# A transformer layer with mixture of experts: the first ada columns on TensorE, x turned and projected in two halves

## The reference

```
c_act = silu(c)                                   # 1024 values
mod   = c_act @ ada_w + ada_b                     # 1024 x 6144: sh1, sc1, g1, sh2, sc2, g2
z     = rmsnorm(x, norm1_g) * (1 + sc1) + sh1
xa, ya, u, v = split(z @ w_in, 4)                 # w_in 1024 x 2048, 512 columns each
o_lru = rg_lru(xa, gelu(ya)) ; o_sgu = sgu(gelu(u), gelu(v))
h     = x + g1 * (concat(rmsnorm(o_lru), rmsnorm(o_sgu)) @ w_out)
z2    = rmsnorm(h, norm2_g) * (1 + sc2) + sh2
h     = h + g2 * moe(z2)                          # 32 experts, top 4, 1024 -> 2048 -> 1024
out   = rmsnorm(h, final_g)
```

## Time and profile before

| | us |
|---|---|
| median of 3 runs | 2230.58 |
| lowest and highest | 2229.54, 2233.26 |
| the profiled execution, its own time | 2232.91 |
| its span in the profile | 2231.2 |
| TensorE busy | 2001.2 |
| VectorE, GpSimd, ScalarE busy | 992.8, 538.4, 356.3 |
| mean granted clock of TensorE | 0.955 of full speed |

### The profile page before, as it was taken

How to read it: one execution, slowest core, us unless ns; L and a number is a source line. 1 busy time by engine, 2 the same in 40 slices (tenths; PEclk the granted TensorE clock), 3 DMA queues, 4 the chain that set the end, 5 groups by cost and what they waited for, 6 DMA issues and landing times.

```text
span 2231.2 us, 51505 instructions
## 1 busy us (share of the span) xinstructions
PE 2001.2 (90%) x20191; PEld 827.5 (37%) x20192; DVE 992.8 (44%) x2237; ACT 356.3 (16%) x723; POOL 538.4 (24%) x530
## 2 busy tenths in 40 slices
PE   3988989976999999999998689969999998999994
PEld 3443444432433343433433123413334332434341
DVE  6436645334444444444444233434444443444444
ACT  3025311221101111101011111111010111110112
POOL 2000022032232323232232222232223232232222
PEclk9998999987999999999999889979999999999997
DMA  9222216250536718673599999799999569955355
GB/s 333 97 110 86 85 55 189 113 195 29 182 106 254 255 28 294 227 247 117 180 391 400 399 402 400 253 379 399 391 401 382 197 226 405 387 191 191 96 183 181
DMA packets 128670, 526.37 MB, mean 236 GB/s; under 512 B 17120, under 2 KB 47840, under 8 KB 79488
## 3 DMA queue, kind: packets, MB, share of 16 engines
q1 hardware_dynamic: 95344, 470.39, 53.9%
q0 software_dynamic: 33296, 55.61, 10.8%
HBM read 493.55 MB, written 32.38 MB: 236 GB/s over the span
## 4 chain that ended last, share of the span: by engine, by line
PE 60%; DMA 11%; SPq 2%; issue 1%; DVE 1%; DVEq 1%; ACT 0%; POOLq 0%
PE psum L1106 39%; PE psum L1124 21%; DMA big<-in_exp_w_gu_dram 9%; SPq L426 1%; DMA big<-in_exp_w_down_dram 1%; DVEq L348 1%; DVE r L1655 0%; PE psum L1058 0%; SPq L436 0%; SPq L433 0%; PE psum L1070 0%; DMA acc_rows<-r,scatter_idx 0%; DMA r<-acc_rows 0%; DVE r L1522 0%; DMA r<-hs_rows,gather_idx 0%
## 5 line engine op out<-in xcount | busy, mean ns | idle before, releaser
L1106 PE MATMUL psum<-big,r 128*32 128x512 f32 x9152 | 1023.0, 604 | 53.2 <-DMA big<-in_exp_w_gu_dram 48.3
L1106 PEld LDWEIGHTS psum<-big,r 128*32 128x32 f32 x9152 | 298.1, 111 | 736.3 <-issue 649.8
L1124 PE MATMUL psum<-big,r 128*32 128x256 f32 x9152 | 529.7, 388 | 44.4 <-DVE r L1605 21.6
L611 POOL DMA_INDIRECT acc_rows<-r,scatter_idx x143 | 226.5, 1584 | 945.9 <-DVE r L1613 928.1
L1124 PEld LDWEIGHTS psum<-big,r 128*32 128x32 f32 x9152 | 301.5, 112 | 251.2 <-issue 47.4
L796 ACT ACTIVATE r<-r,shift 128x128 f32<-128x128 f32 x384 | 157.4, 480 | 1074.5 <-PE psum L1106 891.9
L1590 DVE TENSOR_TENSOR r<-psum,r 128x256 f32<-128x256 f32 x143 | 60.4, 423 | 412.9 <-PE psum L1106 412.7
L603 POOL DMA_INDIRECT r<-hs_rows,gather_idx x196 | 193.8, 989 | 87.0 <-issue 44.7
L1610 DVE TENSOR_TENSOR r<-psum,r 128x256 f32<-128x256 f32 x143 | 60.8, 425 | 339.8 <-PE psum L1124 339.5
L874 PE MATMUL psum<-r,big 128*128 128x512 f32 x384 | 167.9, 598 | 1.3 <-DMA big<-in_w_in_dram 1.3
L803 ACT ACTIVATE r<-r 128x256 f32<-128x256 f32 x143 | 59.6, 417 | 418.3 <-DVE r L1596 416.2
(11 more groups left out here) (233 smaller groups left out, 983.7 us busy)
## 6 DMA issues: line engine op xcount, KB each, us to landing
big<-in_exp_w_gu_dram SPq DMA_DIRECT2D x256, 1024.0 KB
big<-in_exp_w_down_dram SPq DMA_DIRECT2D x128, 1024.0 KB
big<-in_ada_w_dram SPq DMA_DIRECT2D x12, 2048.0 KB, 12.8
r<-in_x_dram SPq DMA_DIRECT2D x16, 512.0 KB, 12.5
big<-in_w_in_dram SPq DMA_DIRECT2D x4, 2048.0 KB, 19.0
r<-in_exp_b_gu_dram SPq DMA_DIRECT2D x128, 64.0 KB
big<-in_w_out_dram SPq DMA_DIRECT2D x2, 2048.0 KB, 13.3
hs_rows<-r POOLq DMA_DIRECT2D x8, 512.0 KB, 3.0
```

Of the source, the lines that this page charges most:

```text
L611: pool.indirect_dma_start(acc_quarters, bass.IndirectOffsetOnAxis(ap=scatter_idx[:, u:u + 1], axis=0), y_sb[:, u, :], None, bounds_check=4 ...
L1106: last = pe.matmul(psum[32 * j:32 * j + 32, u, :].rearrange("p (a n) -> p a n", a=2), izT[:, k, u * UNIT:(u + 1) * UNIT], rhs[:, :, 256 * ...
L1124: ins_ = pe.matmul(psum[32 * i:32 * i + 32, 4 + u % 2, 0:256], actT[:, u, f, :], down_slab(f)[:, 256 * i:256 * i + 256], start=(f == 0), s ...
```

## The change

- The ada tiles 0 to 3 are replaced by four pairs: pair j holds rows 256 j to 256 j + 255 of the first 2048 columns, in rows of 8 KB, in the same slot of the ring. TensorE multiplies them: the stationary operand is `cact_cols`, 32 columns of which the first is silu(c) and the rest zero (GpSimd's memset), and the four groups of 512 columns go into the four 32-partition parts of one bank. `gemv_made` is counted by TensorE after each of the pairs 0 to 2, and once more at the next job. VectorE copies the bank; four small matmuls (`mods`) turn its four rows into 16 columns, and VectorE adds ada_b.
- SyncE issues x 0 to 3, then w_in 0, then x 4 to 7, then ada 4.
- ScalarE squares four tiles of x (into `x_sq`, in `r2`), evicts its half of zT of the first half of tokens, and then does the same for the second half.
- TensorE turns the first half of x, projects xa of the first half, turns the second half and projects it.
- VectorE scales x 0 between its two steps on mod, x 1 to 3 after `scale1`, evicts, scales x 4 to 7, copies the four xa banks of the first half and evicts the second half. The copies of the second half stay where the copies were, with the convolution and the products of ada 4 and 5 between them.

```diff
--- before.py
+++ after.py
@@ -69,10 +69,10 @@
 
 def bank_jobs():
 
-    jobs = [("cols", 0, "dve")]
-    jobs += [("mod", j, "dve") for j in range(4)]
-    jobs += [("zT", (k, th), "dve" if k % 2 else "act") for th in range(2) for k in range(KT)]
-    jobs += [("xa", (m, th), "dve") for m in range(CT) for th in range(2)]
+    jobs = [("cols", 0, "dve"), ("ada", 0, "dve"), ("mods", 0, "dve")]
+    for th in range(2):
+        jobs += [("zT", (k, th), "dve" if k % 2 else "act") for k in range(KT)]
+        jobs += [("xa", (m, th), "dve") for m in range(CT)]
     jobs += [("mod", j, "dve") for j in (4, 5)]
     jobs += [("g1row", q, "dve") for q in range(2)]
     jobs += [("wm", q, "dve") for q in range(2)]
@@ -157,6 +157,9 @@
         def ring(key):
             return big[:, DENSE_AT[key] % DENSE_SLOTS, :].rearrange("p (k n) -> p k n", k=8)
 
+        def ada_pair(j):
+            return big[:, j, :].rearrange("p (k n) -> p k n", k=2)
+
         lru_t = big[:, 4, :].rearrange("p (i n) -> p i n", i=4)
         s5 = big[:, 5, :]
         ln_g = s5[:, 0:512]
@@ -167,6 +170,7 @@
         wi_bd = s5[:, 3072:3584].rearrange("p (c n) -> p c n", c=CT)
         router_w = s5[:, 3584:3840].rearrange("p (k e) -> p k e", k=KT)
 
+        x_sq = r2[:, 5120:6144]
         zT = r1[:, :].rearrange("p (k n) -> p k n", k=KT)
         h_rows = r1[:, :].rearrange("p (t n) -> p t n", t=TT)
 
@@ -219,7 +223,8 @@
         before = lru_t[:, 0, 0:P]
         prow = r2[:, 0:P]
         cols = sb("cols", [P, NROWS])
-        cact = sb("cact", [P, KT])
+        cact_cols = sb("cact_cols", [P, KT, UNIT])
+        cact = cact_cols[:, :, 0]
         mod = sb("mod", [P, 48])
         scale1 = sb("scale1", [P, KT])
         affine2 = sb("affine2", [P, 2, KT])
@@ -402,8 +407,8 @@
                 sp_.dma_start(prow[ROW[name]:ROW[name] + rows, :], src.rearrange(pat, p=P)).then_inc(param_in, SEMW)
 
             for n, (kind, j) in enumerate(DENSE):
-                if n == DENSE_SLOTS:
-                    for t in range(TT):
+                if n in (DENSE_SLOTS, DENSE_SLOTS + 1):
+                    for t in range(4 * (n - DENSE_SLOTS), 4 * (n - DENSE_SLOTS) + 4):
                         sp_.dma_start(x_rows[:, t, :], x[t * P:(t + 1) * P, :]).then_inc(x_in[t], SEMW)
                 if n >= DENSE_SLOTS:
                     old, i = DENSE[n - DENSE_SLOTS]
@@ -412,6 +417,11 @@
                     else:
                         last = ("v", TT - 1) if i == 3 else (("xa", "ya", "u")[i], (CT - 1, 1))
                         sp_.wait_ge(filled, JOB[last] + 1)
+                if n < DENSE_SLOTS:
+
+                    sp_.dma_start(ada_pair(j), ada_w[2 * P * j:2 * P * (j + 1), 0:2048].rearrange("(k p) n -> p k n", p=P)
+                                  ).then_inc(dense_in[n], SEMW)
+                    continue
                 w = {"ada": ada_w, "win": w_in, "wout": w_out}[kind]
                 sp_.dma_start(ring((kind, j)), w[:, j * 512:(j + 1) * 512].rearrange("(k p) n -> p k n", p=P)
                               ).then_inc(dense_in[n % DENSE_SLOTS], SEMW)
@@ -491,6 +501,7 @@
                 ins_.then_inc(pool_chain, 1)
                 pool.wait_ge(pool_chain, chain[0])
 
+            link(pool.memset(cact_cols[:, :, :], 0.0))
             link(pool.memset(ident[:, :], 0.0))
             link(pool.affine_select(out=ident[:, :], in_=ident[:, :], compare_op=ALU.not_equal, fill=1.0, base=0,
                                     pattern=[[-1, P]], channel_multiplier=1))
@@ -667,16 +678,17 @@
 
             act.wait_ge(const_made, 1)
             act.wait_ge(dve_drained, 1)
-            act.activation(cact[:, :], cols[:, ROW["c"]:ROW["c"] + 8], ACT.Silu).then_inc(cact_made, 1)
-
-            for t in range(TT):
-                act.wait_ge(x_in[t], SEMW)
-                link(act.activation(r1[:, 0:D], x_rows[:, t, :], ACT.Square, accum_out=ssum[:, t:t + 1]))
-                act.activation(srt[:, t:t + 1], ssum[:, t:t + 1], ACT.Sqrt, bias=eps[:, 0:1], scale=1.0 / D
-                               ).then_inc(sqrt_made, 1)
-
-            act.wait_ge(affine_made, 1)
+            act.activation(cact, cols[:, ROW["c"]:ROW["c"] + 8], ACT.Silu).then_inc(cact_made, 1)
+
             for th in range(2):
+                for t in range(4 * th, 4 * th + 4):
+                    act.wait_ge(x_in[t], SEMW)
+                    link(act.activation(x_sq, x_rows[:, t, :],
+                                        ACT.Square, accum_out=ssum[:, t:t + 1]))
+                    act.activation(srt[:, t:t + 1], ssum[:, t:t + 1], ACT.Sqrt, bias=eps[:, 0:1], scale=1.0 / D
+                                   ).then_inc(sqrt_made, 1)
+                if th == 0:
+                    act.wait_ge(affine_made, 1)
                 for k in range(0, KT, 2):
                     b = take("zT", (k, th))
                     act.activation(zT[:, k, th * 512:(th + 1) * 512], b, ACT.Identity, bias=mod[:, SH1 + k:SH1 + k + 1],
@@ -880,8 +892,24 @@
             pe.wait_ge(const_made, 1)
             b = open_bank("cols", 0)
             pe.transpose(b[:, 0:NROWS], prow[0:NROWS, :], ident[0:NROWS, 0:NROWS]).then_inc(filled, 1)
-            for j in range(4):
-                mod_cols(j)
+            b = open_bank("ada", 0)
+            pe.wait_ge(cact_made, 1)
+            for n in range(4):
+                dense_ready(("ada", n))
+                for kk in range(2):
+                    k = 2 * n + kk
+                    for i in range(4):
+                        last = pe.matmul(b[32 * i:32 * i + 32, :], cact_cols[:, k, :], ada_pair(n)[:, kk, 512 * i:512 * i + 512],
+                                         start=(k == 0), stop=(k == KT - 1), skip_group_check=True)
+                last.then_inc(gemv_made if n < 3 else filled, 1)
+            b = open_bank("mods", 0)
+            wait_drained(pe, JOB[("ada", 0)])
+            for i in range(4):
+                last = pe.matmul(b[:, 4 * i:4 * i + 4], gacc[:, 0, i * P:(i + 1) * P], ident[:, 0:P:UNIT],
+                                 start=(i == 0), stop=True, skip_group_check=True)
+                if i == 0:
+                    last.then_inc(gemv_made, 1)
+            last.then_inc(filled, 1)
 
             for th in range(2):
                 pe.wait_ge(x_scaled, 4 * th + 4)
@@ -890,11 +918,10 @@
                     for i in range(4):
                         last = pe.transpose(b[:, i * P:(i + 1) * P], x_rows[:, 4 * th + i, k * P:(k + 1) * P], ident[:, :])
                     last.then_inc(filled, 1)
-            dense_ready(("win", 0))
-            for who, drained in (("act", act_drained), ("dve", dve_drained)):
-                pe.wait_ge(drained, drained_before(JOB[("zT", (KT - 1, 1))], who))
-            for m in range(CT):
-                for th in range(2):
+                dense_ready(("win", 0))
+                for who, drained in (("act", act_drained), ("dve", dve_drained)):
+                    pe.wait_ge(drained, drained_before(JOB[("zT", (KT - 1, th))], who))
+                for m in range(CT):
                     project("xa", ("win", 0), m, th)
             for j in (4, 5):
                 mod_cols(j)
@@ -1213,7 +1240,7 @@
 
                 n = DENSE_AT[("ada", j)]
                 dve.wait_ge(dense_in[n % DENSE_SLOTS], SEMW * (n // DENSE_SLOTS + 1))
-                if j >= 2:
+                if j >= 6:
 
                     dve.wait_ge(filled, JOB[("mod", j - 2)] + 1)
                 w, a = ring(("ada", j)), gacc[:, j % 2, :]
@@ -1230,16 +1257,20 @@
                 dve.tensor_tensor(mod[:, 4 * j:4 * j + 4], b[:, 0:4], col("ada_b", 4 * j, 4), ALU.add
                                   ).then_inc(dve_drained, 1)
 
+            def scale_x(t):
+
+                dve.wait_ge(sqrt_made, t + 1)
+                link(dve.reciprocal(rstd[:, t:t + 1], srt[:, t:t + 1]))
+                dve.tensor_scalar(x_rows[:, t, :], x_rows[:, t, :], rstd[:, t:t + 1], None, ALU.mult).then_inc(x_scaled, 1)
+
             dve.wait_ge(cact_made, 1)
-            mod_products(0)
-            mod_products(1)
-            mod_add(0)
-            mod_products(2)
-            mod_add(1)
-            mod_products(3)
-            mod_add(2)
-            mod_add(3)
-            dve.wait_ge(dve_drained, drained_by(JOB[("mod", 3)])[1])
+            b = take("ada", 0)
+            dve.tensor_copy(gacc[:, 0, :], b).then_inc(dve_drained, 1)
+            scale_x(0)
+            b = take("mods", 0)
+            dve.tensor_tensor(mod[:, 0:16].rearrange("p (i b) -> p b i", b=4), b[:, 0:16].rearrange("p (b i) -> p b i", b=4),
+                              col("ada_b", 0, 16).rearrange("p (i b) -> p b i", b=4), ALU.add).then_inc(dve_drained, 1)
+            dve.wait_ge(dve_drained, drained_by(JOB[("mods", 0)])[1])
             link(dve.tensor_scalar(scale1[:, :], mod[:, SC1:SC1 + 8], 1.0, None, ALU.add))
             dve.tensor_tensor(scale1[:, :], scale1[:, :], col("norm1_g", 0, 8), ALU.mult).then_inc(affine_made, 1)
```

(20 more changed lines are left out.)

## The result

| | before | after |
|---|---|---|
| median, timed side by side (22 runs each) | 2231.91 us | 2236.53 us |
| lowest and highest of after | | 2230.61, 2240.80 |
| ratio, 95% interval | | 1.0017 [1.0010, 1.0025] |
| the profiled execution, its span | 2232.91, 2231.2 | 2237.03, 2235.3 |
| mean granted clock | 0.955 | 0.949 |

The change makes the kernel about 4 us slower, and the time lies above the forecast range. The first rows are from the page of after: busy times and the chain, to be set beside the earlier trace rows. VectorE lost the ada products, TensorE got them.

A forecast was written before the change was run, and what follows sets the result against it. TensorE bounds the kernel, its front bytes and then TensorE; 48.3 + 1.7 + 27.5 + 4.5 + 27.5 = 109.5 us against 109.30, +0.2 us, makes the median 2230.8 us. Range 2226.0 to 2234.5.

The forecast's parts named there:

- The bytes: Loads of the front: ada pair 3 lands at 28.3 us, w_in 0 at 48.3, which sets the first projection's start.
- The second rival: In the front's loads, w_in 0 loses to GpSimd's transfers: start at 50.3 us, +3.3 us, 2233.9; chance 0.08.
- The clock there: At the first projection: TensorE idles about 3 us, then half clock loses 1.7 us, with 0 and 2.8 as ends.
- The turn: Between the two halves' projections: transposing the second half costs TensorE 4.5 us, 3.5 transposes and 1.0 wait.
- the third rival: Between the halves, the clock drops at the turn, costing 3.4 us more: +2.9 us, 2233.5; chance 0.14.
- the first: At the first projection, the clock stays high and the first half is ready early: -2.5 us, 2228.1; chance 0.24.
- the fourth: In the front, w_in 0 is issued or lands no earlier than x 7: +5.5 us or more, 2236; chance 0.04.
- VectorE afterwards: Beneath the second half's projections: VectorE's 18.1 us of work ends ahead of the last one, with 2.5 us of cover.
- The front's sum: Start of `mod_cols(4)`: 48.3 + 1.7 + 27.5 + 4.5 + 27.5 = 109.5 us where 109.30 stood, +0.2 us.
- The failed step: Everything behind the front: it keeps its order and moves with the front's end; a difference over 3 us would refute this.
- The range: Whole kernel's time: 2226.0 to 2234.5 us, from the first rival less 2 us to the fourth less 2.

The follow-up runs named there:

- clean_after: The changed kernel with 172 semaphore increments that nobody waits for, all in TensorE's idle time: 2229.13 us, ratio 0.9988 to the kernel before.
- after_again: The changed kernel run once more, nothing altered: 2235.41 us, ratio 1.0023 to the kernel before.
- best: The changed kernel with 60 idle-time semaphore increments on TensorE, and GpSimd's transfers waiting for w_in 0 to land: 2226.36 us, ratio 0.9980 to the kernel before.
- best_free: clean_after with GpSimd's ada transfers also waiting for ada pair 2 and w_in 0 to land: 2227.56 us, ratio 0.9979 to the kernel before.
- free_after: The changed kernel with 60 semaphore increments that nobody waits for in TensorE's idle time: 2232.55 us, ratio 1.0009 to the kernel before.

## Why the prediction was wrong

Point by point, by its own steps:

- **The bytes**: right. Pair 3 at 27.55 (28.3 forecast; the 8 KB rows ran at 422 GB/s in 7.5 to 28 us, not at 403), w_in 0 at 48.15 (48.3). SyncE's queue did not lose to GpSimd's by its shorter rows: 3.03 MB in 31 to 47 us beside 2.47 MB. The second rival falls.
- **The clock there**: right in after, an idle of 3.5 us, then 3.4 us at 0.50, 1.7 us lost. It isn't a law of the idle: clean_after had 2.97 us and no stretch, and after_again, the same program as after, had 3.43 us and a stretch of 6.8 (47.6 to 54.5 us), which took 3.0 us and not 1.7, more than the 2.8 given as the far end.
- **The turn**: 82.18 - 77.42 = 4.8 us (4.5), of it 1.11 wait. No half-clock stretch came there, in after, after_again or best; the third rival falls, and so do the first and the fourth.
- **VectorE afterwards**: the products of ada 5 ended at 107.2 in after, 2.5 us ahead of `mod_cols(4)`: the forecast cover.
- **The front's sum**: 109.5 forecast, 109.72 measured.
- **The failed step** is in the first paragraph: "all behind it follows in one order and moves with it". From `mod_cols(4)` to the end it took 2125.6 us where it had taken 2121.9, and the prediction had named a difference of over 3 us as its refutation. What the runs showed in its place: the order is the same, but not the traffic and not the time. With 32 ada matmuls and 4 small ones in the place of 16 column sums TensorE has more instructions, the packets of its code fall elsewhere, and one falls into the load of w_out 1; the stretch from there to the loop took 181.0 to 183.5 us in the changed kernel's three executions, where the kernel before took 179.9 and 180.1. The prediction has no term for the queue of instructions. The other part, some 3 us from the loop on, has no known cause.
- **The range**: its upper end, "the fourth less 2", is 2234 from a fourth of 2236, not 2234.5. It has no room for the 3 us of scatter on the slow side, nor for a loss behind the front. That the measured 2236.5 is the fourth rival's number is chance: w_in 0 came as forecast.
- **The scatter**: from `mod_cols(4)` to w_out it took 232.1 to 237.1 us in these fourteen executions, the loop 1672.6 to 1678.6; one trace against one therefore can't price 4 us.

What is shown: an instruction packet in the load of w_out 1 goes with a wait of 1.5 to 2.3 us instead of 0.4 to 0.7, in all twenty profiled executions, short kernels included, in the old order of the front as in the new; and the new order is slower than before only with it. Its visible price, up to the loop, is 1 to 3.6 us, by whether the clock drops behind it. That it costs the whole kernel as much is argued and not shown. What stays open: why the loop takes some 3 us more in the changed kernel (executions with the packet took 1702.9 to 1710.1 us from the loop on, those without 1702.9 to 1704.9, so the two overlap); what the rest of clean_after's 6 to 7 us is (the other packets moved as well, and the stretch behind 49 us went); why best and best_free, with and without the packet, are even in 12 and 11 runs although the profiled spans are 2.8 us apart; and why free_after's packet moved so little. No kernel here moves that one packet alone, since all packets move together.

## What to carry to other kernels

Take the instruction queue into the account when an edit changes how many instructions an engine has: a load that just fits beneath its cover can be made late by code fetched for work that comes afterwards, and a part that the edit never touched can lose what the edited part breaks even on. Compare the parts of a run one by one, and in more than one execution each: here the two first profiles put the whole loss into the loop, and the repeats only about half. When a change moves a stage's start, ask which loads behind it have less than 2 us to spare, and look at every queue in their windows. And where two queues share the DMA engines, hold the bytes that nobody needs yet behind the one tile that TensorE waits for: here that one changed wait gave 6.2 us, and with 2226.4 us the fastest kernel, best_free's 2227.6 aside, which noise can't tell from it.

## What the hardware showed that was not expected

- What is taken for TensorE's code comes in packets of 16,384 bytes on a queue of its own (q8 in the trace), 15 or 16 in this kernel, each taking mostly 0.9 to 1.4 us. w_out 1, beside which nothing but the tiles of x behind it in the same queue was moving, landed its sixteen parts over 1.3 to 2.3 us where it met one, over 0.4 to 0.7 where it did not.
- Loads on SyncE's queue alone ran at 422 GB/s with rows of 8 KB in 7.5 to 28 us, where 2 KB rows had 390 and 4 KB rows 410. The Trainium skill (DMA: Bandwidth & Descriptors, Queues, rings and completion order) has each engine go round robin by packets; between the 2 KB rows of w_in 0 and GpSimd's transfers no run here shows the loss that one would take from it (3.03 MB for SyncE's queue in 16 us, 2.66 before).
- A pair of ada took TensorE 1.92 us at the high level (clean_after, 27.55 us) and 3.4 at the low one (after_again, 27.46 us, at 0.50 for all but its end), 1.7 and 3.4 forecast from line 1106. The first pair took 3.64, where the trace has no record of the clock yet.
